# A hybrid decoder layer: state-space steps in another order, sample states from one product of 96 stacked rows

## The chip, the cores and the metric

The kernel runs on one core of a Trainium2 chip. A time is the device time of one execution in microseconds (us); a lower one is better. The engines are TensorE (PE; its weight loads are shown as PEld), VectorE (DVE), ScalarE (ACT), GpSimd (POOL) and SyncE (SP). Each takes its instructions in order, and they wait for one another by semaphores.

## What is computed

One layer of a decoder for a prompt of 512 tokens and 8 sequences of 8 new tokens each (64 sample tokens with a cache of 1024 positions and a state). Everything is fp32. Cut to what matters here:

```
h = rmsnorm(x);  q,k,v,z,xbc,dt,ga,gb = split(h @ w_in)
attn = stick_breaking_attention(q, k, v, cache)
xs,B,C = split(silu(causal_conv(xbc)))          # 32 heads of 64, 4 groups with 128 states each
per chunk of 128 tokens (samples: per sequence of 8):
    y_diag = (C B^T * L) (x dt)                 # L = exp of segment sums, lower triangle
    h      = h * decay + (x dt * decay_to_end)^T B
    y_off  = C h_before * exp(a_cum)
y = rmsnorm((y_diag + y_off + d_skip * xs) * silu(z), per group)
merged = sigmoid(ga) * (attn @ w_pa) + sigmoid(gb) * (y @ w_pb)
x = x + merged @ w_out;  x = x + (silu(h2 @ w_gate) * (h2 @ w_up)) @ w_down     # h2 = rmsnorm(x)
```

Among the outputs are the new states of the 8 sample sequences, `ssm_sample`: for each sequence, head and group, old state times decay plus the sum over its 8 tokens of `x dt decay` times `B`.

## The kernel before

The program is written as one stream of instructions for each engine, in the functions under `with` blocks for SP, POOL, PE, ACT and DVE; the order on each engine is the order of its Python code, and a table `keys`/`use` gives each product that is not a weight product one of four PSUM banks in turn (`spare`). All 576 tokens (512 + 64) go through each weight product at once.

A weight product keeps fp32 exactness by splitting: each operand is a hi part in fp32r and a lo part (the rest). `product` (L434 to L448) does three matmuls for each of two halves of 288 columns: w_hi x_hi (L443), w_hi x_lo (L444), w_lo x_hi (L447). One slice is 128 rows of the contraction, six matmuls; a tile is eight slices for 128 output columns, and a chunk of weights is one tile (two for w_pb). For each chunk ACT makes the hi part (L411) and DVE the lo part (L417).

The stages are: projections of q, k, v; attention, with the projections of the gates and some z tiles as filler (`Z_EARLY` lists the z tiles made there, kept in DRAM and brought back); w_pa; then the state-space part (from 483 us), w_out and the feed-forward part. The state-space part goes over four groups g of 8 heads. `by_token(g)` on PE transposes the convolved xs into five token blocks (`x_tok`, L1258; DVE makes `xdt` = x dt from each, L2291), B into `b_tok`, and forms C B^T (`cb`); slices of one weight tile (`key_after`, called `around` by the caller) stand between these. Then come the steps c = 0 to 3, one for each chunk of the prompt, and c = NC (4) for the samples. In a prompt step PE does:

- `segments` (L1292, L1293, L1300): segment sums by a product with picks; ACT takes exponentials (L1856) into `decay`;
- `old_and_state`: L1311 is the part of the output from the old state; L1318 the chunk's new state from `xend` (x dt decay_to_end, made by DVE at L2323);
- `new_outputs` (L1329): the output from the same chunk, from `decay` times C B^T (DVE, L2316) and `xdt`;
- `turn_old` (L1340) and twice `sequence(g, b)`: L1349 is the output of sample sequence b from its old state (8 columns), L1357 the addition to its state, which multiplies `xend_s` (64 sample tokens) by `b_seq[:, b]`, B with all tokens zero but those of b. `b_seq` is made by POOL (L882), `xend_s` by DVE (L2307). Before, this product is plain fp32.

Between these stand slices of filler tiles. `ssd_plan(g)` lists for each step two lists of tiles, and at its end those around the gate's sums of squares (`y_ss`, L1408): tiles of z (`z`), of the next group's inputs (`into`) or of w_pb for the group before (`pb`, two weight tiles in one). `step_tiles` makes `one` and `two` of them. With two tiles, four slices of `one` stand before `old_and_state` and four after it, and two of `two` at each of the four places behind. With one tile, three slices stand before, and one at each of the five places behind.

After a group, y is gated by z, squared (ACT), summed (PE, L1408) and scaled (DVE); ACT makes its hi part `y_hi` (L1937), DVE its lo part `y_lo` (L2426), from which the w_pb tiles of the next group's steps read. Behind the last group PE transposes the convolution's last rows (`conv_out`, L1422), which ACT copies out, and does the last w_pb tiles (`last_pb`); DVE then forms `merged` (L2439 to L2446).

On DVE, `prepare(g, c)` is what the change moves most. It waits until ACT has read both segment banks, multiplies `decay` by C B^T, then makes `xend`:

```
wait_after_read(eng, ("seg", g, c, q))          # q = 0, 1
eng.tensor_tensor(decay[...], decay[...], cb_m[...], ALU.mult)      # L2316
eng.tensor_tensor(xend[...], xdt[:, c], end_decay[...], ALU.mult)   # L2323
```

## Time and profile before

| | |
|---|---|
| median of 3 runs | 1569.98 us (1564.76, 1569.98, 1571.89) |
| profiled execution | 1569.13 us, its span 1567.6 us |
| PE busy | 1471.1 us, 94% of the span |
| DVE, ACT, POOL busy | 816.9, 635.5, 214.4 us |
| mean granted clock of TensorE | 0.971 |

The page says of which engine the busy time is; the views by stretch add the mean granted clock of the same stretch (1.00 is the full clock, 0.50 half of it). In the timelines, a row is an instruction or several alike in a row: its start, its time (start of the first to end of the last), engine, line, and in brackets how long the engine stood idle before it and for whom. Times of neighbouring matmuls overlap; the distance between starts is the time that each takes from PE.

### The profile page before, as it was taken

Reading aid. Unit: us, or ns where it says so; the run is one execution under the profiler, and the core shown is the slowest. Engines: PE = TensorE matmul, PEld = TensorE weight load, DVE = VectorE, ACT = ScalarE, POOL = GpSimd, SP = SyncE. Lnnn points to the kernel's source line nnn. Section 1 sums busy time; section 2 is a strip of 40 time slices with the busy share of each in tenths; the row PEclk is TensorE's granted clock in tenths of the full one; section 3 lists DMA queues with packets and bytes.
Section 4 is the critical chain, followed back from the end, with each engine's and each line's share of the span. In section 5 each row is a group of like instructions: output and inputs, shape, how many; then the busy total and the mean of one; then the engine's idle time right before and its main releaser. Section 6 shows DMA issues by size and latency. Waiting matters only on the chain. (4 is left out here: it accounts for less than half of the span.)

```text
span 1567.6 us, 27375 instructions
## 1 busy us (share of the span) xinstructions
PE 1471.1 (94%) x10773; PEld 1376.9 (88%) x10773; DVE 816.9 (52%) x1174; ACT 635.5 (41%) x1049; POOL 214.4 (14%) x391
## 2 busy tenths in 40 slices
PE   4998999999899998999999999979999999999997
PEld 4997778888799887979988988869999999999997
DVE  3454556878723655567666674546444444442221
ACT  4574446666513424534444353233433332322121
POOL 3011231000112122122112212111200000000001
PEclk9999999999999998899999999989999999999999
DMA  4235673222375232333333424354222322223331
GB/s 111 82 97 152 187 216 98 64 64 64 91 187 122 83 102 74 96 95 101 82 103 103 107 61 115 86 154 145 68 82 80 93 80 80 80 80 92 95 97 46
DMA packets 201110, 157.37 MB, mean 100 GB/s; under 512 B 13672, under 2 KB 187216, under 8 KB 200959
## 3 DMA queue, kind: packets, MB, share of 16 engines
q1 hardware_dynamic: 175394, 97.93, 22.1%
q0 software_dynamic: 25232, 57.70, 13.2%
q8 instruction: 67, 1.10, 0.3%
q10 hardware_dynamic: 384, 0.37, 0.1%
q14 instruction: 33, 0.27, 0.1%
HBM read 132.04 MB, written 23.91 MB: 99 GB/s over the span
## 5 line engine op out<-in xcount | busy, mean ns | idle before, releaser
L443 PE MATMUL tile_banks<-x_hi,w_hi 128*128 128x288 f32 (+1 forms) x1808 | 537.4, 311 | 20.1 <-ACT gate_out L1686 14.4
L444 PE MATMUL tile_banks<-x_lo,w_hi 128*128 128x288 f32 (+1 forms) x1808 | 512.1, 298 | 0.0
L447 PE MATMUL tile_banks<-x_hi,w_lo 128*128 128x288 f32 (+1 forms) x1808 | 391.2, 298 | 0.0
L443 PEld LDWEIGHTS tile_banks<-x_hi,w_hi 128*128 128x128 f32 (+1 forms) x1808 | 344.8, 191 | 36.9 <-issue 26.5
L444 PEld LDWEIGHTS tile_banks<-x_lo,w_hi 128*128 128x128 f32 (+1 forms) x1808 | 345.3, 191 | 4.8 <-issue 3.6
L417 DVE TENSOR_TENSOR w_lo<-w_raw,w_hi 128x1024 fp32r<-128x1024 f32 (+2 forms) x169 | 206.8, 1224 | 172.7 <-ACT w_hi L411 171.6
L447 PEld LDWEIGHTS tile_banks<-x_hi,w_lo 128*128 128x128 f32 (+1 forms) x1808 | 293.8, 190 | 0.4
L411 ACT ACTIVATE w_hi<-w_raw 128x1024 fp32r<-128x1024 f32 (+2 forms) x169 | 175.7, 1039 | 104.7 <-PE tile_banks L447 104.4
L443 PE MATMUL tile_banks<-f_hi,w_hi 128*128 128x288 f32 x352 | 99.4, 297 | 0.0
L444 PE MATMUL tile_banks<-f_lo,w_hi 128*128 128x288 f32 x352 | 98.5, 295 | 0.0
L443 PE MATMUL tile_banks<-y_hi,w_hi 128*128 128x288 f32 x256 | 79.8, 326 | 8.7 <-DVE merged L2439 8.7
L447 PE MATMUL tile_banks<-f_hi,w_lo 128*128 128x288 f32 x352 | 75.6, 296 | 0.0
L444 PE MATMUL tile_banks<-y_lo,w_hi 128*128 128x288 f32 x256 | 74.7, 306 | 0.0
L444 PEld LDWEIGHTS tile_banks<-f_lo,w_hi 128*128 128x128 f32 x352 | 66.3, 188 | 0.0
L443 PEld LDWEIGHTS tile_banks<-f_hi,w_hi 128*128 128x128 f32 x352 | 66.2, 188 | 0.0
L1800 ACT ACTIVATE conv_src<-tile_banks 128x288 f32<-128x288 f32 x24 | 9.9, 411 | 138.8 <-PE tile_banks L447 138.8
L1986 ACT ACTIVATE f_hi<-prod 128x576 f32 (+1 forms) x22 | 15.1, 686 | 119.9 <-DVE prod L2477 119.9
L443 PEld LDWEIGHTS tile_banks<-y_hi,w_hi 128*128 128x128 f32 x256 | 50.8, 198 | 14.3 <-DVE w_lo L417 9.1
L944 POOL DMA_DIRECT2D out_y_prompt<-y_tok x8 | 6.3, 785 | 416.4 <-ACT y_tok L1999 416.4
L2255 DVE SCALAR_TENSOR_TENSOR conv_acc<-conv_src,conv_par,conv_acc 128x600 f32<-128x600 f32 x72 | 60.8, 844 | 2.5
L447 PEld LDWEIGHTS tile_banks<-f_hi,w_lo 128*128 128x128 f32 x352 | 56.4, 188 | 0.0
L447 PE MATMUL tile_banks<-y_hi,w_lo 128*128 128x288 f32 x256 | 56.3, 302 | 0.0
(355 smaller groups left out, 2470.7 us busy)
## 6 DMA issues: line engine op xcount, KB each, us to landing
w_raw<-in_w_in SPq DMA_DIRECT2D x68, 512.0 KB, 4.0
w_raw<-in_w_gate SPq DMA_DIRECT2D x22, 512.0 KB, 3.8
w_raw<-in_w_up SPq DMA_DIRECT2D x22, 512.0 KB, 3.9
k_page<-in_cache_k SPq DMA_DIRECT2D x64, 128.0 KB, 2.6
v_page<-in_cache_v POOLq DMA_DIRECT2D x64, 128.0 KB, 2.9
old<-in_state_ssm POOLq DMA_DIRECT2D x32, 256.0 KB, 3.4
out_ssm_sample<-old POOLq DMA_DIRECT2D x32, 256.0 KB, 2.7
w_raw<-in_w_pb SPq DMA_DIRECT2D x16, 512.0 KB, 4.0
```

What stands on the lines that cost most here:

```text
L411: nc.scalar.activation(w_hi[:, c % 2, 0:tiles, 0:width], w_raw[:, c % 2, 0:tiles, 0:width], ACT.Copy).then_inc(hi_made, 1)
L417: nc.vector.tensor_tensor(w_lo[:, c % 2, 0:tiles, 0:width], w_raw[:, c % 2, 0:tiles, 0:width], f32(w_hi[:, c % 2, 0:tiles, 0:width]), ALU. ...
L443: nc.tensor.matmul(out, wh, xh[:, HALVES[h]], start=start and k == 0, stop=False, skip_group_check=onto)
L444: nc.tensor.matmul(out, wh, xl[:, HALVES[h]], start=False, stop=False, skip_group_check=onto)
L447: mm = nc.tensor.matmul(out, wl, xh[:, HALVES[h]], start=False, stop=stop and k == last, skip_group_check=onto)
L944: eng.dma_start(y_prompt[0].rearrange("(c p) n -> p c n", p=P)[:, :, bass.ds(P * i, P)], y_tok[:, 0:NC, :]).then_inc(sem("y_out"), 16)
L1800: eng.activation(dst[:, 3:3 + HALF], G[t % 2][:, 0, 0:HALF], ACT.Copy)
L1986: eng.activation(f_hi[:, bass.ds(2 * i + n, 1), :], prod2[:, n:n + 1, :], ACT.Copy).then_inc(sem("f_hi_made"), 1)
L2255: ins = eng.scalar_tensor_tensor(out=dst, in0=src[:, w:w + m], scalar=conv_par[:, w * CT + ct:w * CT + ct + 1], in1=dst, op0=ALU.mult, op1 ...
```

## The change

Two sets of edits go together.

1. **Sample states.** B of the samples and `xend_s` are split into hi and lo parts of fp32r and stacked on 96 partitions: 32 sample tokens (four sequences) three times, B as hi, hi and lo, `xend_s` as hi, lo and hi (lo, hi and hi for the second four), so one product of 96 rows gives the three partial products' sum. ACT makes the hi parts of B by six copies of 32 rows, DVE the lo parts by two subtractions; POOL's `spread_b` makes `b_seq` for four sequences at a time, so twice in a group (the second at c = 2, after the fourth sequence's product). `xend_f` is the fp32 product, ACT copies its hi parts (`xend_hi`, four copies of 32x512 behind the segments of c = 0), DVE subtracts (`xend_lo`, two of 32x512 behind the outputs of c = 0).
2. **Order.** `make_xend` is taken out of the end of `prepare`: for c = 0 it stands in `by_token` behind the second xdt, for the others at the start of `prepare`. Four slices of `around` stand before `by_token` instead of two, then 2, 1 and 1 between. `Z_EARLY` and `ssd_plan` share out z and w_pb tiles anew: in group 0, z(0,2) is made at c = 0 and c = 1 has two tiles; after groups 1 and 2 one z tile fewer is done; in the last group pb2 stands before the sums of squares and pb3 behind them. The last group's y_hi and y_lo have buffers of their own (over y_t and z_s). `a_seq` is made earlier on POOL, in the space of `conv_out`, and `picks` is narrower by one block.

```
-    Z_EARLY = [(0, 1), (0, 2), (1, 2), (1, 3), (2, 2), (2, 3)]
+    Z_EARLY = [(0, 1), (1, 2), (1, 3), (2, 1), (2, 2), (2, 3)]
...
 # ssd_plan: g == 0
-   [([z[3]], [into[0]]), ([into[1]], []), ([into[2]], []), ([into[3]], []), ([into[4]], [into[5]]), ([("z",1,0)], [("z",1,1)])]
+   [([z[2]], [into[0]]), ([z[3]], [into[1]]), ([into[2]], []), ([into[3]], []), ([into[4]], [into[5]]), ([("z",1,0)], [("z",1,1)])]
 # g = 1, 2: the last entry
-   ([pb[3]], [("z", g + 1, 0), ("z", g + 1, 1)])
+   ([pb[3]], [("z", g + 1, 0)])
 # g = 3
-   [([z[2]], []), ([z[3]], [pb[0]]), ([], [pb[1]]), ([], [pb[2]]), ([], []), ([pb[3]], [])]
+   [([z[1]], []), ([z[2]], [pb[0]]), ([z[3]], []), ([pb[1]], []), ([], []), ([pb[2]], [pb[3]])]
...
 # POOL, spread_b(g, n), called with n = 0 before the steps and n = 1 at c == 2
+   eng.tensor_tensor(b_seq[:, :, :], f32(b_hl[:, n, :]).unsqueeze(1).to_broadcast([3 * ROWS, SEQS, P]),
+                     in_seq_3[:, :].unsqueeze(2).to_broadcast([3 * ROWS, SEQS, P]), ALU.mult)
...
 # PE, by_token
-   gemm(key_after, {1: range(2, 4), 3: range(4, 6), 4: range(6, 8)}[c])
+   gemm(key_after, {1: range(4, 6), 3: range(6, 7), 4: range(7, 8)}[c])
 # PE, sequence
-   mm = pe.matmul(spare(key)[:, j * P:(j + 1) * P], xend_s[:, 2 * j:2 * j + 2, :]..., b_seq[:, b, :], ...)
+   mm = pe.matmul(spare(key)[:, j * P:(j + 1) * P], xend_s[:, b // SEQS, 2 * j:2 * j + 2, :]..., b_seq[:, b % SEQS, :], ...)
 # PE, end of a group
-   for key in later[:-1]:
+   for key in later if last else later[:-1]:
        gemm(key)
-   around = later[-1] if later else None
-   gemm(around, range(0, 2))
+   around = None if last else later[-1]
+   gemm(around, range(0, 4))
...
 # ACT, by_token and xend_hi
-   eng.activation(b_tok[0:TS, NC, :], spare(key)[0:TS, 0:P], ACT.Copy)
+   for n in range(2):
+       for k in (2, 1, 0):
+           ins = eng.activation(b_hl[k * ROWS:(k + 1) * ROWS, n, :], spare(key)[n * ROWS:(n + 1) * ROWS, 0:P], ACT.Copy)
...
+       for at in (n * ROWS, 2 * ROWS):
+           ins = eng.activation(xend_s[at:at + ROWS, n]..., rows, ACT.Copy)
 # ACT, sequence
+   if b == 1:
+       eng.wait_ge(sem("xend_s_made"), g + 1)
...
 # DVE, prepare
+   if 0 < c < NC:
+       make_xend(g, c)
    (waits for the segments, decay times C B^T)
-   if c < NC:
-       eng.tensor_tensor(xend[:, :, :], xdt[:, c], end_decay[...], ALU.mult)
```

The three places below show the order that the engines' streams have; the names are the tiles, as in `out<-in`.

DVE, `by_token` of group 1 and the decay product of its step c = 0, before:

```order
L2291 TENSOR_TENSOR xdt<-spare_bank,dt_tok 128x512 [waits bank_full0,y_split,bank_read0,conv_done]
L2291 TENSOR_TENSOR xdt<-spare_bank,dt_tok 128x512 [waits bank_full1]
L2291 TENSOR_TENSOR xdt<-spare_bank,dt_tok 128x512 [waits bank_full2]
L2291 TENSOR_TENSOR xdt<-spare_bank,dt_tok 128x512 [waits bank_full3]
L2291 TENSOR_TENSOR xdt<-spare_bank,dt_tok 64x512 [waits bank_full0]
L2295 TENSOR_SCALAR y_t<-xs_t,par 128x576 x4
L2299 TENSOR_TENSOR cb_m<-spare_bank,upto 128x512 [waits bank_full2]
L2303 TENSOR_TENSOR cb_m<-spare_bank,upto_b 64x64 [waits b_tok_made]
L2307 TENSOR_TENSOR xend_s<-xdt,end_decay 64x512 [waits bank_full0,bank_read0]
L2316 TENSOR_TENSOR decay<-decay,cb_m 128x1024 [waits bank_read2,bank_read1,bank_read0]
L2323 TENSOR_TENSOR xend<-xdt,end_decay 128x512 [waits bank_full1,bank_read0]
```

The same place in the changed kernel (`old_t` in its tenth row is the space that `xend_f` takes):

```order
L2336 TENSOR_TENSOR xdt<-spare_bank,dt_tok 128x512 [waits bank_full1]
L2324 TENSOR_TENSOR xend<-xdt,end_decay 128x512 [waits bank_full1,bank_read0]
L2336 TENSOR_TENSOR xdt<-spare_bank,dt_tok 128x512 [waits bank_full2]
L2336 TENSOR_TENSOR xdt<-spare_bank,dt_tok 128x512 [waits bank_full3]
L2336 TENSOR_TENSOR xdt<-spare_bank,dt_tok 64x512 [waits bank_full0]
L2342 TENSOR_SCALAR y_t<-xs_t,par 128x576 x4
L2346 TENSOR_TENSOR cb_m<-spare_bank,upto 128x512 [waits bank_full2]
L2352 TENSOR_TENSOR b_hl<-spare_bank,b_hl 32x128 [waits b_hi_made]
L2352 TENSOR_TENSOR b_hl<-spare_bank,b_hl 32x128
L2354 TENSOR_TENSOR cb_m<-spare_bank,upto_b 64x64
L2358 TENSOR_TENSOR old_t<-xdt,end_decay 64x512 [waits bank_full0,bank_read0]
L2379 TENSOR_TENSOR decay<-decay,cb_m 128x1024 [waits bank_read2,bank_read1,bank_read0]
```

xend moved from behind the decay product to behind the second xdt, and two subtractions stand ahead of the sample part.

PE, `by_token` of group 1, between the fourth and the fifth transposition of x_tok (L1258), before:

```order
L443 MATMUL tile_banks<-x_hi,w_hi 128x288
L444 MATMUL tile_banks<-x_lo,w_hi 128x288
L443 MATMUL tile_banks<-x_hi,w_hi 128x288
L444 MATMUL tile_banks<-x_lo,w_hi 128x288
L447 MATMUL tile_banks<-x_hi,w_lo 128x288 x2
L443 MATMUL tile_banks<-x_hi,w_hi 128x288
L444 MATMUL tile_banks<-x_lo,w_hi 128x288
L443 MATMUL tile_banks<-x_hi,w_hi 128x288
L444 MATMUL tile_banks<-x_lo,w_hi 128x288
L447 MATMUL tile_banks<-x_hi,w_lo 128x288 x2
L1258 MATMUL spare_bank<-ident,xs_t 64x128 [waits bank_read0]
L1258 MATMUL spare_bank<-ident,xs_t 64x128 x3
```

The same place in the changed kernel:

```order
L451 MATMUL tile_banks<-x_hi,w_hi 128x288
L452 MATMUL tile_banks<-x_lo,w_hi 128x288
L451 MATMUL tile_banks<-x_hi,w_hi 128x288
L452 MATMUL tile_banks<-x_lo,w_hi 128x288
L455 MATMUL tile_banks<-x_hi,w_lo 128x288 x2
L1279 MATMUL spare_bank<-ident,xs_t 64x128 [waits bank_read0]
L1279 MATMUL spare_bank<-ident,xs_t 64x128 x3
```

One slice instead of two stands ahead of the fifth transposition, which waits until DVE has read the first one's bank.

PE, the end of the last group, from the last sum of squares (L1408), before:

```order
L1408 MATMUL spare_bank<-conv_acc,ones 128x288 [waits y_squared]
L1408 MATMUL spare_bank<-conv_acc,ones 128x288
L1422 MATMUL spare_bank<-ident,conv_out 27x128 [waits bank_read3,conv_tails]
L1422 MATMUL spare_bank<-ident,conv_out 27x128 x3
L1422 MATMUL spare_bank<-ident,conv_out 27x128 [waits bank_read0]
L1422 MATMUL spare_bank<-ident,conv_out 27x128 x3
```

The same place in the changed kernel:

```order
L1429 MATMUL spare_bank<-conv_acc,ones 128x288 [waits y_squared]
L1429 MATMUL spare_bank<-conv_acc,ones 128x288
L451 MATMUL tile_banks<-y_hi,w_hi 128x288 [waits tile_free0,y_split,weights_split]
L452 MATMUL tile_banks<-y_lo,w_hi 128x288
L451 MATMUL tile_banks<-y_hi,w_hi 128x288
L452 MATMUL tile_banks<-y_lo,w_hi 128x288
```

The two tiles of pb3 now stand between the sums of squares and the transposes of the convolution's rows.

## Rows read from the trace of the kernel before

**Rows 1.** Stretches of groups 0, 1 and 3: busy time by engine, granted clock.

```profile
core 0: us, PE busy (x) PEld busy (x) DVE busy (x) ACT busy (x) POOL busy (x), PEclk, DMA share, GB/s
546.70:677.90 131.20, 122.74 (x789) 107.95 (x788) 76.03 (x127) 56.40 (x95) 25.90 (x43) 0.87 0.31 86
677.90:806.70 128.80, 125.07 (x933) 114.24 (x931) 85.06 (x138) 56.26 (x95) 25.38 (x43) 1.00 0.37 99
...
936.00:1073.00 137.00, 121.42 (x834) 108.66 (x834) 78.06 (x128) 45.67 (x67) 28.61 (x43) 0.91 0.43 128
```

**Rows 2.** PE's waits, 470 to 1075 us: total us, times, longest us.

```profile
PE spare_bank L1318 <- DVE xend L2323: 9.3, 9, 2.7
PE tile_banks L443 <- DVE merged L2439: 8.7, 2, 6.0
PE tile_banks L443 <- DVE w_lo L417: 4.5, 2, 2.3
PE spare_bank L1422 <- ACT xdt L1943: 4.2, 1, 4.2
PE spare_bank L1258 <- ACT xs_t L1773: 3.8, 1, 3.8
PE spare_bank L1216 <- POOL e_t L854: 2.6, 1, 2.6
PE spare_bank L1258 <- DVE xdt L2291: 2.5, 1, 2.5
```

**Rows 3.** Short stretches around falls of the clock; columns as in rows 1.

```profile
580.32:583.73 3.41, 3.41 (x28) 3.27 (x29) 2.26 (x6) 0.00 (x0) 0.00 (x0) 1.00 0.30 82
583.73:590.55 6.82, 6.82 (x24) 4.97 (x23) 2.90 (x8) 2.44 (x5) 2.77 (x5) 0.50 0.39 115
617.86:621.28 3.42, 3.13 (x8) 2.13 (x8) 0.74 (x2) 0.00 (x0) 0.00 (x0) 0.50 0.00 0
628.10:641.76 13.66, 13.66 (x55) 12.16 (x55) 7.02 (x14) 5.99 (x11) 2.93 (x6) 0.50 0.33 93
1030.88:1037.70 6.82, 5.79 (x26) 5.49 (x27) 3.68 (x5) 4.41 (x8) 2.09 (x4) 0.50 0.11 22
```

**Rows 4.** Timeline of PE, end of a slice and one sample sequence: start, us.

```profile
560.65 0.43 PE L447 MATMUL tile_banks<-x_hi,w_lo 128*128 128x288 f32 x2
560.92 0.95 PE L1349 MATMUL spare_bank<-bc_t,old_t 128*128 128x8 f32 x8
561.80 1.16 PE L1357 MATMUL spare_bank<-b_seq,xend_s 64*128 64x128 f32 x8
562.88 0.40 PE L443 MATMUL tile_banks<-x_hi,w_hi 128*128 128x288 f32 x1
```

**Rows 5.** Timeline of PE in attention, fp32r products of 128 columns.

```profile
278.12 0.22 PE L1164 MATMUL tile_banks<-wt_hi,v_hl 128*128 128x128 f32 x1
278.17 0.28 PE L1164 MATMUL tile_banks<-wt_lo,v_hl 128*128 128x128 f32 x1
278.29 0.44 PE L1164 MATMUL tile_banks<-wt_hi,v_hl 128*128 128x512 f32 x1
```

**Rows 6.** Timeline of all engines, group 0, step c = 3.

```profile
616.17 1.23 DVE L2316 TENSOR_TENSOR decay<-decay,cb_m 128x1024 f32<-128x1024 f32 x1 [2.46 <-ACT decay L1856]
...
617.32 0.68 DVE L2323 TENSOR_TENSOR xend<-xdt,end_decay 128x512 f32<-128x512 f32 x1
...
618.15 1.19 PE L1318 MATMUL spare_bank<-xend,b_tok 128*128 128x512 f32 x1 [2.74 <-DVE xend L2323]
```

**Rows 7.** Groups of instructions by form: count, busy us, mean ns, idle before.

```profile
L1824 ACT ACTIVATE b_tok<-spare_bank 64x128 f32<-64x128 f32 x4 | 1.1, 270 | 2.2 <-PE spare_bank L1277 2.2
...
L2307 DVE TENSOR_TENSOR xend_s<-xdt,end_decay 64x512 f32<-64x512 f32 x4 | 9.4, 2361 | 0.0
...
L882 POOL TENSOR_TENSOR b_seq<-b_tok,in_seq 64x1024 f32<-64x1024 f32 x4 | 7.6, 1888 | 77.7 <-ACT b_tok L1824 52.7 <-issue 25.0
```

**Rows 8.** Timeline of DVE, the last group's y_lo.

```profile
1030.58 2.76 DVE L2426 TENSOR_TENSOR y_lo<-y_t,y_hi 128x576 fp32r<-128x576 f32 x4
```

More of the change, by code:

```diff
@@ L503, in last_sums, with y_parts @@
             return ("e", g, c) if c else ("seg", g, c, 1)
+        def y_parts(g):
+            return (y_hi, y_lo) if g < NG - 1 else (y_last_hi, y_last_lo)
         def src_tile(key):
@@ L751, in _ @@
             rule(in_seq[:, :], 1.0, [(ge, 0, [[-TD, NB]], 1), (ge, TD - 1, [[TD, NB]], -1)], 0.0)
+            for k in range(3):
+                put(eng.tensor_copy, in_seq_3[k * ROWS:(k + 1) * ROWS, :], in_seq[0:ROWS, 0:SEQS])
             sem_const_all.append(n_made[0])
@@ L1241, in gemm @@
                         w = [a[:, c % 2].rearrange("p t n -> p (t n)")[:, cols] for a in (w_hi, w_lo)]
-                        x = (y_hi[:, k, :], y_lo[:, k, :])
+                        x = [y[:, k, :] for y in y_parts(key[1])]
                     else:
@@ L1832, in pick_group @@
                     eng.activation(sums[0:2 * NH, TP:T], one[:, 0:TS], ACT.Copy)
-                    for e in range(2):
-                        other = T + e * P + (1 - e) * HD
-                        eng.activation(picks[0:2 * NH, other:other + HD], one[:, 0:HD], ACT.Copy, scale=0.0).then_inc(sem("sums_filled"), 1)
-                    eng.wait_ge(sem("sums_filled"), 2)
+                    eng.activation(picks[0:2 * NH, T + HD:T + P], one[:, 0:HD], ACT.Copy, scale=0.0).then_inc(sem("sums_filled"), 1)
+                    eng.wait_ge(sem("sums_filled"), 1)
                     eng.wait_ge(sem("sums_split"), 4)
@@ L2280, in empty, with make_xend @@
                         ins.then_inc(tile_free[(t + n) % 2], 1)
+            def make_xend(g, c):
+                wait_after_read(eng, ("x_tok", g, c))
+                n = g * NC + c
+                if n:
+                    wait_full(eng, ("state", (n - 1) // NC, (n - 1) % NC))
+                eng.tensor_tensor(xend[:, :, :], xdt[:, c], end_decay[:, c, g * HG:(g + 1) * HG].unsqueeze(2).to_broadcast([P, HG, HD]), ALU.mult)\
+                   .then_inc(sem("xend_made"), 1)
             def by_token(g):
@@ L2301, in by_token @@
                 key = ("sample_bc", g)
-                eng.wait_ge(sem("b_tok_made"), g + 1)
+                eng.wait_ge(sem("b_hi_made"), g + 1)
+                low = slice(2 * ROWS, 3 * ROWS)
+                for n in range(2):
+                    ins = eng.tensor_tensor(b_hl[low, n, :], spare(key)[n * ROWS:(n + 1) * ROWS, 0:P], f32(b_hl[low, n, :]), ALU.subtract)
+                ins.then_inc(sem("b_split"), 1)
                 eng.tensor_tensor(cb_m[0:TS, NC, 0:TS], spare(key)[0:TS, P:P + TS], upto_b[:, :], ALU.mult).then_inc(bank_read[use[key][0]], 1)
@@ L2306, in by_token, with xend_lo @@
                     wait_full(eng, ("new_state", g - 1, NB - 1))
[L2307 to L2308 removed]
+                eng.tensor_tensor(xend_f.rearrange("p (h d) -> p h d", h=HG), xdt[0:TS, NC],
+                                  end_decay[0:TS, NC, g * HG:(g + 1) * HG].unsqueeze(2).to_broadcast([TS, HG, HD]),
+                                  ALU.mult).then_inc(sem("xend_f_made"), 1)
+            def xend_lo(g):
+                eng.wait_ge(sem("xend_hi_made"), g + 1)
+                for n in range(2):
+                    rows, other = slice(n * ROWS, (n + 1) * ROWS), slice((1 - n) * ROWS, (2 - n) * ROWS)
+                    flat = [x.rearrange("p h d -> p (h d)") for x in (xend_s[other, n], f32(xend_s[rows, n]))]
+                    ins = eng.tensor_tensor(flat[0], xend_f[rows, :], flat[1], ALU.subtract)
+                ins.then_inc(sem("xend_s_made"), 1)
             def prepare(g, c):
                 m = P if c < NC else TS
+                if 0 < c < NC:
+                    make_xend(g, c)
                 for q in range(2):
@@ L2317, in prepare @@
                    .then_inc(sem("decay_made"), 1)
-                if c < NC:
-                    wait_after_read(eng, ("x_tok", g, c))
-                    n = g * NC + c
-                    if n:
-                        wait_full(eng, ("state", (n - 1) // NC, (n - 1) % NC))
-                    eng.tensor_tensor(xend[:, :, :], xdt[:, c], end_decay[:, c, g * HG:(g + 1) * HG].unsqueeze(2).to_broadcast([P, HG, HD]), ALU.mult)\
-                       .then_inc(sem("xend_made"), 1)
             def outputs(g, c):
@@ L2425, in _ @@
                     eng.wait_ge(sem("y_hi_made"), PG * g + j + 1)
-                    ins = eng.tensor_tensor(y_lo[:, j, :], y_t[:, j, :], f32(y_hi[:, j, :]), ALU.subtract)
+                    high, low = y_parts(g)
+                    ins = eng.tensor_tensor(low[:, j, :], y_t[:, j, :], f32(high[:, j, :]), ALU.subtract)
                 ins.then_inc(sem("y_split"), 1)
```

83 lines of the change are left out of this document (53 added, 30 removed).

## The prediction, made before the changed kernel was run

> **What bounds the kernel now.** I read the stretches of the four state-space groups first, since all but one of the edits lie there. TensorE (PE) is the bound: in the stretch of group 0 it is busy 122.74 of 131.20 us, and in that of group 1 125.07 of 128.80 [rows 1]. So PE loses time in three ways: in waits, in the time its own instructions take, and in the granted clock. The clock column shows the last: 0.87 in group 0 and 0.91 in the last group, but 1.00 in group 1 [rows 1]. The levels are 2.4 and 1.2 GHz, so 0.87 over 131.20 us means 2 x 0.13 x 131.20 = 34 us at half speed, which costs 17 us; 0.91 over 137 us means 25 us, which costs 12. Second, PE's waits [rows 2]: the largest is 9.3 us in nine waits of L1318 (a chunk's new state) for xend, which VectorE (DVE) makes behind the decay product. Third, the low stretches [rows 3]. Some come behind a wait, as at 617.86. Others do not: from 580.32 to 583.73 PE is busy in all 3.41 us at 1.00, and the next 6.82 us run at 0.50 with PE busy throughout. That happens in steps with one filler tile, where the 8-column products of L1349 and the 64-row products of L1357 stand closest together. The stretch at 583.73 is one of three alike; the one at 628.10 is 13.66 us long.
>
> **The product of the sample states (L1357).** It is 4 fp32 matmuls for each of 8 sequences in 4 groups, and each matmul leaves two records. In the timeline the first of 8 records starts at 561.80 and the next tile's slice at 562.88 [rows 4]: 1.08 us for a sequence, 0.135 a record. The new form is 4 fp32r matmuls of 128 columns with 96 rows, one record each. No row shows 96 rows. The nearest are the fp32r products of the same 128 columns in attention: a 128-column one starts at 278.12, the next at 278.17, and a 512-column one at 278.29 [rows 5], so 0.05 and 0.12 us. I take 0.11, near the upper, because here the weights change with each matmul as at 278.17; it is also what an 8-column record at L1349 takes, (561.80 - 560.92)/8 = 0.11 [rows 4]. So 4 x 0.11 = 0.44 us, and the saving is (1.08 - 0.44) x 32 = **20.5 us**. The bounds: nothing faster per record than 0.135 gives 17.3 us; 0.05 gives 28. The work is on PE's path, so what it saves is seen unless a wait takes it. The Trainium skill's page "TensorE: Matmul & The Clock Gate" (section "Back-to-back issue gap") states about 81 ns a matmul for a stream of 128-column matmuls each with its weight load; by that figure an estimate is 0.32 us a sequence and 24 us in all. The two rows stand on both sides of it.
>
> **xend moved ahead of the decay product.** At 616.17 DVE starts the decay product (1.23 us), 2.46 us late because ScalarE (ACT) made the exponentials; xend follows at 617.32, and PE starts L1318 at 618.15 after a wait of 2.74 [rows 6]. xend needs neither. Moved ahead, it is ready long before, and L1318 would start at 615.41. PE then has one slice of six matmuls (0.135 each, 0.8 us [rows 4]) behind L1318's 0.55 and waits at L1329 for the decay product, which ends at 617.4 (by 616.17 + 1.23): 617.4 - 616.75 = 0.65 us. The other eight waits come to 6.6 us, 0.8 each; there the decay product, which now starts with the exponentials and no later than before, ends before PE has done L1318 and its slices. At c=0 of groups 1 to 3 I leave 0.9 in two of them, because there more work stands ahead of it (below). So of 9.3 us some 2.5 stay: **-6.8**.
>
> **What is added in a group.** ACT copies the hi parts of B in six instructions of 32x128 instead of one of 0.270 us [rows 7], so by that row some 1.35 us more stand ahead of the exponentials of c=0; its four copies for xend come after these and ahead of the next weight chunk. DVE has two small subtractions in by_token and two of 32x512 after the outputs of c=0; the step's xend of 0.685 us now lies between the second and third xdt. GpSimd (POOL) makes b_seq in two halves. Before, its one instruction of 1.888 us lies beside DVE's xend_s, which takes 2.361 although a full 128x512 product takes 0.68 (617.32 in [rows 6]); the two slow each other. POOL's first half is half as long; the second half comes at c=2, where I charge DVE up to 1 us, hidden by a step's slices. That half waits on POOL for the fourth sequence's product; queued behind it are the next sums and the old states of c=3, which are wanted a step later. ACT's copy for the second sequence waits for the split of xend, with c=0's slices between. DVE is busy 76 of 131 us and ACT 56 [rows 1], so I cost all this at nothing outside by_token and c=0. There the cover is the slices of `around` and of one or two tiles; if that cover is gone each group pays up to 2 us. The Trainium skill's page "SBUF — State Buffer" (section "Who interferes with whom") says that a DVE instruction with two SBUF inputs and a GpSimd instruction that reads SBUF exclude each other for a whole instruction. The trace agrees (2.361 beside 1.888 [rows 7]); by it the second half costs DVE about 1 us, and the sum would not change as long as DVE is not late there.
>
> **The start of a group.** Two more slices stand ahead of the first transposes of x_tok and one fewer between the fourth and the fifth. In group 0 the wait of 3.79 us for xs_t (L1258, [rows 2]) has 1.6 us more work ahead of it: -1.7 with rounding. In group 1 the wait of 2.45 for xdt shrinks by 1.6 - 0.8: -0.8. In groups 2 and 3 the end of the group before loses a whole tile of 6.4 us, and the fifth transposition will wait for DVE as long as the two waits for w_lo (4.5 in all [rows 2]) do now: zero. Sum **-2.5**. a_seq made early is worth little: the wait of 2.6 at L1216 is put down to it, but ACT's signed sums, on which the same product depends, come hardly earlier. **-0.5**, at most 2.6.
>
> **The end of the last group.** Before, the tile pb3 stands ahead of the sums of squares, and behind them PE has only the convolution rows' transposes, which wait 4.23 us at L1422 [rows 2]; around that the clock is at 0.50 for 6.82 us with 5.79 busy [rows 3], which costs 2.9. Now pb3's 6.4 us stand behind the sums, and the whole chain of the gate starts 6.4 us earlier. y_hi and y_lo get buffers of their own, so they need not wait for pb3. DVE's y_lo (2.76 us from 1030.58 [rows 8]) then would end at 1026.9, and the low part of the next weights, 1.2 us after it, sets the first tile of last_pb at about 1028.6, where it was 1033.5. **-5**; bounds 0 and 4.23 + 2.9 = 7.1. Next late there is the old wait for `merged` (8.7 us in two, [rows 2]), which the change leaves.
>
> **The clock.** The stretch at 617.86 goes with its wait: -1.7. That at 583.73 is in step c=1 of group 0, which has a second tile now: -3.4. The other one-tile stretches (6.8 for 628.10, 3.4 each for the other two) may stay or go: the steps are as they were, but the product that ran in them is shorter and the slices stand closer. I take half: -6.8. Sum **-12**; bounds: the whole 29 us of the two columns gone (17 + 12, of which the tail's 2.9 is counted above), and a clock that is worse than now.
>
> **The sum.** -20.5 - 6.8 - 2.5 - 0.5 - 5 - 12 = -47.3. The profiled execution took 1569.13 us (span 1567.6, the rest lies around it), the median of the runs is 1569.98. 1569.13 - 47.3 = 1521.8, and against the median 1522.7: **1523 us**.
>
> **Rivals.**
> (a) The clock is not regained: the one-tile steps keep what they have, or fall in all seven (there are two in group 0, one each in groups 1 and 2, three in group 3) for 6.82 us each. That is 7 x 3.4 = 24 us instead of the 17 of now: with the waits' own 1.7 regained, 1523 + 10 to 1523 + 17, so 1533 to 1540. For it: 583.73, where a wholly busy PE fell. Against it: the clock of 1.00 in group 1, whose step c=0 has one tile too. The Trainium skill, "TensorE: Matmul & The Clock Gate" (section "What's actually happening"), has the level follow how busy the array has been recently. By that rule removing waits raises the clock, and shorter products without more work behind them do not; the fall at 583.73 without a wait is not what its text alone leads one to expect.
> (b) ACT and DVE become the bound in by_token and at c=0. The six copies and the two subtractions delay the decay product by 2 us in each group: 1523 + 8 = 1531. For it: in before the exponentials already come 2.46 us late once [rows 6].
> (c) The product's price is the bound of either side: 0.135 a record gives 1526, 0.05 gives 1516.
> (d) The change does not do what it says with the waits: each simply moves from L1318 to L1329, and the by_token gain goes: 1523 + 9 = 1532.
> (e) The other side: with the fp32 product gone, every one of the 16 prompt steps runs low for 13.66 us as at 628.10. That costs 16 x 6.83 = 109 us against 17 in such steps now, +92, and leaves 1569 + 92 - 35 = 1626, slower. It decides from 17 + 35 = 52 us, that is, from eight of the 16 steps. Against it: nine steps have two tiles, and group 1 has a clock of 1.00 now.
>
> **How the numbers follow.** Forecast (1515 to 1530) 0.45; (a) 0.20; (b) 0.10; (c) 0.12, of which half below 1517; (d) 0.05; (e) 0.04; 0.04 for partial mixes that end within 0.5%, which is about what a measurement of this kernel can tell from no change. The low end takes in (c) at 0.05 with most of the clock back, 1505; the high end (a) with (b), 1546. Faster by over 0.5%: 0.92; within: 0.04; slower: 0.04.
>
> **What would show it.** L1357's successor has 128 records, about 0.11 us apart; if 0.135 or 0.05, (c). The waits of L1318 are gone, and L1329 waits under 1 us in a few places; if the waits are as large as before, (d); if L1329 waits about 2 us at c=0 of each group, (b). The 4.23 us at L1422 are gone, those for `merged` remain. The clock of group 0's stretch rises from 0.87 to about 0.93, with no low stretch in its step c=1; if it stays under 0.90, (a). The prediction is wrong in its core if PE's waits in the four groups do not fall by at least 10 us, or if the groups' clock falls.

## The result and the profile after

The changed kernel takes 1515.24 us (median of four runs, 1509.8 to 1519.96) where the kernel before takes 1570.93 in the same job: a ratio of 0.965 with a 95% interval of 0.9603 to 0.9697, 56 us less. A second set of runs of the same program gave 1512.63 us and 0.9653 (0.9612 to 0.9694). The prediction was 1523 us with a range of 1505 to 1546. The profiled execution took 1519.96 us, its span 1518.5, so 49 us less than the profiled one of before.

The changed kernel has other line numbers: L1318 (the new state from xend) is L1339, L1329 (the outputs that need the decay product) is L1350, L1258 is L1279, L1340 (the transposes of the samples' old states) is L1361, L1349 and L1357 are L1370 and L1378, L1422 is L1444.

The stretches of the four groups, each from its first segment sums to those of the next, the last one to the start of w_out (busy time by engine, granted clock; columns as in [rows 1]). The last row is the only stretch of over 7 us at half speed there:

```profile
541.04:652.02 110.98, 107.42 (x805) 97.05 (x803) 78.28 (x129) 61.45 (x105) 28.17 (x44) 1.00 0.38 106
652.02:768.74 116.72, 114.18 (x854) 104.21 (x852) 85.78 (x145) 58.86 (x102) 25.75 (x45) 0.99 0.38 108
768.74:885.08 116.34, 112.73 (x853) 102.97 (x852) 84.56 (x138) 59.22 (x103) 24.04 (x42) 1.00 0.36 100
885.08:1024.53 139.45, 125.80 (x842) 114.58 (x841) 80.75 (x135) 53.13 (x78) 28.81 (x44) 0.88 0.44 131
895.05:912.11 17.06, 16.91 (x67) 15.01 (x68) 6.49 (x14) 7.62 (x9) 3.63 (x5) 0.50 0.38 103
```

Group 0 took 131.20 us at a clock of 0.87 [rows 1] and takes 110.98 at 1.00, although it does a z tile more (z(0,2)). Groups 1 and 2 do one z tile less each (6.4 us of their 12 and 13). The last group gained nothing in this execution: its stretch went from 137.00 to 139.45, since a whole z tile moved into it and the clock fell to 0.50 for 17 us.

PE's waits from 470 us to the start of w_out (total us, times, longest us), to be read against [rows 2] and two smaller rows of the kernel before, which come first:

```profile
PE spare_bank L1349 <- DVE state L2361: 1.2, 5, 0.3
PE spare_bank L1329 <- DVE decay L2316: 1.0, 1, 1.0
```

```profile
PE tile_banks L451 <- DVE merged L2498: 9.4, 2, 6.4
PE spare_bank L1279 <- DVE xdt L2336: 5.4, 3, 1.9
PE spare_bank L1361 <- DMA old<-in_state_ssm: 3.4, 3, 1.9
PE spare_bank L1350 <- DVE decay L2379: 2.3, 4, 1.1
PE spare_bank L1244 <- ACT decay L1773: 2.2, 1, 2.2
PE spare_bank L1279 <- ACT xs_t L1795: 2.1, 1, 2.1
PE spare_bank L1370 <- DVE state L2417: 0.9, 4, 0.2
PE spare_bank L1339 <- DVE xend L2324: 0.9, 1, 0.9
PE tile_banks L451 <- DVE pb_sum L2315: 0.4, 1, 0.4
PE spare_bank L1339 <- ACT decay L1888: 0.4, 1, 0.4
PE spare_bank L1429 <- ACT conv_acc L1956: 0.2, 1, 0.2
```

The 9.3 us for xend are 0.9, the 4.2 us at the convolution rows are gone, the two waits for w_lo too. New is a wait of 3.4 us in three places for the old states of the samples (L1361). `merged` stays. All these waits together were 37.8 us and are 27.6.

The timeline of one sample sequence (start, us), as [rows 4] showed it before:

```profile
554.64 0.95 PE L1370 MATMUL spare_bank<-bc_t,old_t 128*128 128x8 f32 x8
555.45 0.64 PE L1378 MATMUL spare_bank<-b_seq,xend_s 96*128 96x128 f32 x4
555.92 0.35 PE L451 MATMUL tile_banks<-x_hi,w_hi 128*128 128x288 f32 x1
```

From the first record of the product to the next slice pass 0.47 us, where it was 1.08.

### The profile page after: what moved, and what is told of

Same layout as the page of the kernel before. It is cut to its first block and busy times, and to the rows that moved or that the text cites. A ratio compares the mean times of both kernels' runs of the same rounds, so it can differ in the third digit from the quotient of the medians.

```text
span 1518.5 us, 27179 instructions
## 1 busy us (share of the span) xinstructions
PE 1435.1 (95%) x10645; PEld 1348.8 (89%) x10645; DVE 823.0 (54%) x1190; ACT 654.2 (43%) x1086; POOL 217.2 (14%) x398
## 3 DMA queue, kind: packets, MB, share of 16 engines
q8 instruction: 66, 1.08, 0.3%
## 5 line engine op out<-in xcount | busy, mean ns | idle before, releaser
L451 PE MATMUL tile_banks<-y_hi,w_hi 128*128 128x288 f32 x192 | 57.6, 314 | 0.0
L777 POOL DMA_DIRECT2D v_page<-in_cache_v x64 | 34.5, 538 | 161.2 <-issue 161.2
L452 PE MATMUL tile_banks<-y_lo,w_hi 128*128 128x288 f32 x192 | 54.3, 298 | 0.0
L2162 DVE TENSOR_TENSOR_SCAN after_w<-rest,zero_col 128x128 f32<-128x128 f32 (+2 forms) x64 | 52.3, 818 | 0.3
```

What stands on the lines that cost most here:

```text
L451: nc.tensor.matmul(out, wh, xh[:, HALVES[h]], start=start and k == 0, stop=False, skip_group_check=onto)
L452: nc.tensor.matmul(out, wh, xl[:, HALVES[h]], start=False, stop=False, skip_group_check=onto)
L777: eng.dma_start(v_page[:, n % V_SLOTS, :], cache_v[0, bass.ds(page_of(eng, x, k), 1)].rearrange("o p h d -> p (o h d)")).then_inc(sem(f"v_ ...
L2162: link(eng.tensor_tensor_scan(out=after_w[:, slot, edge - width:edge][:, ::-1], data0=rest[:, slot, cols][:, ::-1], data1=zero_col[:, 0:1] ...
```

## Experiments

All times are medians; the kernels of one job share its runs of the kernel before (1567 to 1569 us). Each kernel has one profile, the changed kernel two. "Low" is the time at half clock between 500 and 1100 us of the profiled execution, the sum of its stretches; it was 65 us before and 38 after (24 in the second profile of the changed kernel).

### The two halves alone

The product alone: the kernel before with B and xend split, b_seq of 96 rows and

```
-   mm = pe.matmul(spare(key)..., xend_s[:, 2 * j:2 * j + 2, :]..., b_seq[:, b, :], ...)
+   mm = pe.matmul(spare(key)..., xend_s[:, b // SEQS, 2 * j:2 * j + 2, :]..., b_seq[:, b % SEQS, :], ...)
```

> The kernel before with the sample states by the fp32r product of 96 rows, and nothing else changed: xend behind the decay product, the old plans, the old end. Both theories: four records of 0.12 us for a sequence instead of eight of 0.135, so (1.08 - 0.47) x 32 = 19.5 us less on PE, and the old waits (L1318's 9.3 us in nine, 4.2 at the convolution's rows) as they were. Theory A (the fp32 products of 64 rows are what the clock falls behind in steps with one tile): the low stretches of group 0 that follow no wait (17 us at half speed there, 34 in all four groups, 17 us lost) go with them, in all 1571 - 19.5 - 15 = 1536 us, and the granted clock of group 0's stretch is 0.95 or more. Theory B (the steps with one tile themselves, or the waits in them): the stretches stay, 1571 - 19.5 = 1551 us, the clock of group 0 0.90 or less.

Measured: 1550.41 us against 1567.25, 0.9893 (0.9858 to 0.9927): 17 us less, as theory B had it, but not for its reason: the clock of group 0's stretch is 0.96, as theory A had it, and it is the waits that grew. The waits for xend (L1331 is L1318 here) and a few stretches:

```profile
PE spare_bank L1331 <- DVE xend L2364: 17.6, 8, 3.5
```

```profile
569.37:585.69 16.32, 15.17 (x115) 12.94 (x113) 11.42 (x21) 5.67 (x10) 5.09 (x8) 1.00 0.34 96
...
593.44:596.85 3.41, 2.79 (x6) 1.79 (x7) 1.07 (x2) 0.00 (x0) 0.85 (x2) 0.50 0.28 73
613.92:617.33 3.41, 3.04 (x7) 2.04 (x8) 0.82 (x2) 0.00 (x0) 0.00 (x0) 0.50 0.17 56
```

The waits for xend nearly doubled, from 9.3 to 17.6 us: PE comes to L1331 earlier, and xend still stands behind the exponentials and the decay product. At c = 0 it is also later, because six copies of B stand ahead of the exponentials on ACT:

```profile
548.05 1.66 ACT L1839 ACTIVATE b_hl<-spare_bank 32x128 fp32r<-32x128 f32 x6 [0.56 <-PE spare_bank L1290]
549.73 1.28 ACT L1879 ACT_TABLE_LOAD   x1
551.02 1.09 ACT L1879 ACTIVATE decay<-spare_bank 128x512 f32<-128x512 f32 x2
```

So 8 of the 19.5 us went straight into waits, and the clock fell at 593 and 614 around waits of 3.15 and 3.46 us, where before it had fallen in the steps. Group 0's stretches that follow no wait (583.73 in [rows 3]) are gone: step c = 1, the first row above, has the full clock. Low is 58 us in all.

The order alone: the changed kernel with the plain fp32 product.

```
-   eng.wait_ge(sem("b_split"), g + 1);  spread_b(g, 0)
+   eng.wait_ge(sem("b_tok_made"), g + 1);  (one b_seq of 64 rows x 8 sequences, as before)
```

> The changed kernel with the sample states as before (plain fp32 product of 64 rows, one b_seq for a group): order and plans alone. Both theories: L1318's waits fall from 9.3 us to under 3, those at the end of the last group and in by_token by 4 and 2.5, so 13 to 15 us less. Theory A: the stretches at half speed behind fp32 products in one-tile steps stay where a step still has one tile (group 0, c = 2 and 3: 20 us at half speed, so 10 lost), only that of c = 1 and the ones behind long waits go, 5 to 8 us: 1571 - 14 - 7 = 1550 us. Theory B: the waits were the cause, the clock comes back in all of them: 1571 - 14 - 17 = 1540 us, clock of group 0 0.95 or more. If the two edits add up, the two gains together are 56 us (1571 - 1515).

Measured: 1541.55 us, 0.9849 (0.9813 to 0.9886): 26 us less, between the theories (21 and 31 less). No wait for xend is left. But the clock of group 0's stretch is 0.90, and three long stretches at half speed begin in one-tile steps (c = 2 and 3 of group 0, c = 0 of group 1) with PE busy throughout and no wait over 0.26 us next to them; step c = 1 of group 0, which has two tiles here, keeps the full clock:

```profile
542.11:667.53 125.42, 123.15 (x838) 110.33 (x836) 75.54 (x125) 57.44 (x96) 24.97 (x43) 0.90 0.34 94
598.53:612.18 13.65, 13.65 (x51) 11.46 (x51) 7.08 (x15) 6.91 (x12) 4.54 (x8) 0.50 0.46 130
622.42:632.66 10.24, 10.24 (x40) 8.74 (x40) 5.12 (x10) 5.54 (x11) 2.92 (x6) 0.50 0.36 102
680.45:690.69 10.24, 10.24 (x36) 8.08 (x36) 6.79 (x12) 3.52 (x7) 4.50 (x8) 0.50 0.42 115
```

What follows from both: the halves give 17 and 26 us, together 43, and both at once 55 in the same job (1512.63). By the three intervals the 12 us on top can be about 2 to 22. The profiles show where each half alone hands something back: the product alone to waits for xend (8 us more of them, and low stretches around them), the order alone to low stretches in steps with fp32 products (48 us low, against 38 and 24).

### xend taken by itself, and put back

Alone, in the kernel before:

```
+   if 0 < c < NC:
+       make_xend(g, c)          # ahead of the decay product; c = 0 in by_token
    (waits, decay times C B^T)
-   eng.tensor_tensor(xend[:, :, :], xdt[:, c], ...)
```

> The kernel before with one edit: xend made ahead of the decay product (for c = 0 in by_token), all else as before, the sample product in plain fp32. Theory (the wait at L1318 was only for the place of xend on DVE): L1318's 9.3 us in nine waits fall under 1 us, L1329 waits up to 1 us in all, the low stretch behind the longest wait goes (1.7 us), those in one-tile steps stay, since the fp32 products of 64 rows are there: 9 + 2 = 11 us less, 1556 us from 1567. Rival: the wait moves to the decay product (L1329), and the time stays at 1567.

Measured: 1560.94 us, 0.994 (0.9917 to 0.9964): 8 us less. The wait at L1318 is gone in the trace and 0.6 us stand at L1329, so the rival falls: the wait does not move there (1.6 us for old states are new, at L1340 in group 2). The profiled execution, with 89 us low, was the slowest of its four (1571.16; the others 1558 to 1563). Group 0's one-tile steps ran low about as before (27 us of the 31 there), the first two rows; in the last group's steps 34 us were low where it had been 7, the third row for example:

```profile
603.63:613.87 10.24, 10.24 (x36) 8.08 (x36) 5.04 (x10) 6.44 (x12) 4.50 (x8) 0.50 0.45 126
624.11:634.35 10.24, 10.24 (x40) 8.74 (x40) 4.79 (x11) 5.07 (x11) 2.93 (x6) 0.50 0.38 108
982.51:996.16 13.65, 13.65 (x52) 11.47 (x52) 5.45 (x13) 2.73 (x4) 3.02 (x4) 0.50 0.38 112
```

In that execution all that the waits gave went back to the clock; the other three were 8 to 13 us faster than it. Why the last group ran low for longer is not shown. The same edit undone in the changed kernel:

> The changed kernel with xend made behind the decay product again, at the end of prepare. Theory (the two parts are worth more together: the shorter product and the added copies make PE wait longer for xend, as the product alone showed with 17.6 us of such waits): L1318's successor waits 15 to 18 us, five of the waits over 2.5 us, each with a low stretch of 3.4 us or more behind it (1.7 each, 8 in all): 1513 + 15 + 8 = 1536 us. Rival (the parts add up): it costs what xend's waits were before, 1513 + 7 = 1520 us.

Measured: 1531.61 us, 0.9759 (0.9723 to 0.9796): 16 to 19 us more than the changed kernel (1515.24 and 1512.63), with 15.4 us of waits for xend (eight, the longest 2.9), low 51 us. The theory of 1536 is nearer than the rival of 1520. By the medians the same move of one instruction on DVE is worth 8 us in the kernel before (6 to 13 by the interval) and 16 to 19 behind the shorter product (8 to 25); the waits that it removes, 9.3 and 15.4 us, say the same with less noise.

### What the clock falls behind

> The changed kernel with each fp32r product of the sample states done twice (the second overwrites the first with the same values), so that PE spends about as long at that place as with the plain fp32 product: 32 x 0.47 = 15 us more of work. Theory A (what the clock falls behind in one-tile steps is the fp32 product with its 64 rows, not the time that passes between slices): the clock of group 0's stretch stays at 0.97 or more, and the time is 1513 + 15 = 1528 us. Rival (the time between slices decides): stretches at half speed come back in the one-tile steps of groups 0 and 1, 20 to 34 us of them: 1513 + 15 + 10 to 17 = 1538 to 1545 us.

```
-   for j in range(PG):
+   for j in list(range(PG)) * 2:
```

Measured: 1524.06 us, 0.9738 (0.9708 to 0.9769), nearer theory A's 1528 than the rival's 1538 to 1545. Eight fp32r records take PE 0.92 us (556.18 to 557.10), close to the 1.08 of eight fp32 records, and group 0 keeps the full clock:

```profile
541.77:656.32 114.55, 111.01 (x837) 100.60 (x835) 78.28 (x129) 61.44 (x105) 28.18 (x44) 1.00 0.36 103
```

```profile
555.37 0.95 PE L1370 MATMUL spare_bank<-bc_t,old_t 128*128 128x8 f32 x8
556.18 1.09 PE L1378 MATMUL spare_bank<-b_seq,xend_s 96*128 96x128 f32 x8
557.10 0.35 PE L451 MATMUL tile_banks<-x_hi,w_hi 128*128 128x288 f32 x1
```

With the order the same, the fp32 product gave 0.90 and this one 1.00, so in group 0 it is not the time between slices. Over all kernels the clock of group 0's stretch sorts by the product: 0.87 before, 0.89 with xend alone, 0.90 with the order alone; with the fp32r product 0.96 where xend's waits are there (product alone, xend put back), and 0.98 to 1.00 in the others, but for 0.93 in the first of the two runs with the old end below, the one that leaves out slices. Its steps in group 0 are those of the changed kernel, and still its step c = 3 has a low stretch with no wait over 0.23 us in the step:

```profile
542.74:660.10 117.36, 112.60 (x794) 101.20 (x792) 80.00 (x133) 61.56 (x105) 26.75 (x44) 0.93 0.36 100
615.66:622.49 6.83, 6.83 (x27) 5.57 (x27) 4.59 (x9) 5.20 (x11) 2.59 (x6) 0.50 0.49 136
```

Whether it is the type or the 64 rows instead of 96 was not tried apart. Nor is the clock safe with the fp32r product in the last group, which has three one-tile steps. It ran low for 10 and 14 us in the run with the product twice, and for 10 us from 951 in the second profile of the changed one, with no wait over 0.43 us in the steps where that began; the order alone, with the fp32 product, has only 3.4 us low in that group's steps.

```profile
908.96:919.20 10.24, 10.24 (x38) 8.30 (x38) 4.30 (x8) 5.74 (x7) 3.36 (x5) 0.50 0.52 142
966.98:980.63 13.65, 13.04 (x66) 11.62 (x66) 8.51 (x17) 4.04 (x7) 2.27 (x3) 0.50 0.27 85
987.65:991.06 3.41, 3.41 (x15) 3.41 (x16) 3.26 (x6) 2.21 (x4) 0.75 (x1) 0.50 0.06 19
```

The first two rows are of the run with the product twice, the third of the order alone. So what sets the clock is shown for group 0 in part, and for the last group not at all. Over whole executions the mean granted clock was 0.970 to 0.982 with the order alone, 0.982 to 0.984 with the product twice and 0.975 to 0.986 in the changed kernel.

> The changed kernel with z(0,2) made as filler in attention again instead of z(2,1), so that step c = 1 of group 0 has one tile as before (and the end of group 1 has z(2,1)). Theory A (the fp32 products were what the clock fell behind): with the short product the one-tile step c = 1 keeps the full clock: 1513 us, within 3. Rival (the number of tiles decides): a low stretch of 6.8 us or more comes back in c = 1 of group 0, and waits of 1 to 2 us there: 1513 + 3.4 + 2 = 1518 us or more.

```
-   [([z[2]], [into[0]]), ([z[3]], [into[1]]), ...        # g == 0
+   [([z[3]], [into[0]]), ([into[1]], []), ...            # z(0,2) in Z_EARLY, z(2,1) at the end of group 1
```

Measured: 1510.62 us, 0.9645 (0.9608 to 0.9683), no difference from the changed kernel. With one tile again, step c = 1 keeps the clock:

```profile
544.24:649.00 104.76, 101.15 (x758) 90.66 (x756) 76.25 (x128) 60.40 (x104) 28.58 (x44) 1.00 0.38 107
```

So no worth of the sharing out of z tiles in group 0 shows once the product is short. Step c = 1 keeps the clock with either edit alone: with the second tile and the fp32 product in the order alone, with one tile and the fp32r product here and in the product alone.

### The end of the last group

> The changed kernel with the end of the last group as before: pb3 ahead of the sums of squares, y_hi and y_lo of the last group in the shared buffers (step c = 2 of that group takes z3 and pb1, c = 3 takes pb2). Theory: the 4.2 us wait at the convolution rows' transposes comes back with half speed around it: 4.5 to 7 us more, 1518 to 1520 us. Rival: pb3 only moved, and what waits behind it (the first w_pb tile of the last group, merged) takes the time: 1513 us, no change.

This kernel left out part of the work: two slices of one weight tile in each of three groups, 4.8 us. It took 1521.07 us (0.9675). The wait for DVE's xdt was 10.2 us in three, where the slices were missing, so its time doesn't answer the question. With them in place:

> As the run before with the end of the last group put back, but with every slice of the tile around by_token in place: that run left out two slices of one tile in three groups, 6 x 0.8 = 4.8 us of PE's work. Theory: the wait of 4.2 us at the convolution rows' transposes is there with half speed around it, and the changed kernel's waits are otherwise unchanged: 1513 + 4.5 to 7, so 1518 to 1520 us; with the clock as it was in the incomplete run up to 1526. Rival: nothing is gained by moving pb3: 1513 us.

```
-   ([z[3]], []), ([pb[1]], []), ([], []), ([pb[2]], [pb[3]])
+   ([z[3]], [pb[1]]), ([pb[2]], []), ([], []), ([pb[3]], [])
```

Measured: 1518.03 us, 0.9695 (0.9667 to 0.9724), 3 to 5 us more than the changed kernel; the intervals overlap (0.9612 to 0.9694 and 0.9603 to 0.9697), so the size is open, but the wait is back (L1435 is L1444 in the changed kernel):

```profile
977.40 1.91 PE L1435 MATMUL spare_bank<-ident,conv_out 128*27 128x128 f32 x16
983.53 1.91 PE L1435 MATMUL spare_bank<-ident,conv_out 128*27 128x128 f32 x8 [4.23 <-ACT xdt L1970]
```

### The new wait, and what is late next

> The changed kernel with the first two old states of a group loaded on POOL ahead of its wait for the split B, instead of behind the first half of b_seq. In the changed kernel PE waits 3.4 us in three places (0.2, 1.3, 1.86) at the transposes of the old states for these loads. Theory: they are late because they stand behind b_seq on POOL; then the waits go: 3.4 us less, and if the stretch at half speed that begins behind the longest of them (895.05 to 912.11) is its consequence, 8.5 us more: 1503 to 1512 us, clock of the last group's stretch from 0.88 to 0.94. Rival: the loads land no earlier since the states stored by the group before hold their buffers: no change, 1515 us, waits as they are.

```
+   for b in (0, 1):
+       old_states_in(g, b)
    eng.wait_ge(sem("b_split"), g + 1)
    ...
-       if c < NC:
+       if 0 < c < NC:
```

> The changed kernel once more, unchanged, as the ground for the others on the same chip: 1510 to 1520 us, ratio to before 0.960 to 0.970. If the stretch at half speed in step c = 0 of the last group comes by chance, it will be absent or shorter in this profile while the wait of 1.9 us ahead of it is there.

Measured in one job: 1505.45 us with the states first (0.9605, 0.9578 to 0.9631), 1512.63 unchanged (0.9653, 0.9612 to 0.9694). The wait at L1361 is gone from the trace. In the changed kernel PE stops there for what stands in POOL's queue: the first row is b_seq, which waits for the split of B, the second row the loads behind it.

```profile
887.83 1.03 POOL L873 TENSOR_TENSOR b_seq<-b_hl,in_seq 96x512 fp32r<-96x512 f32 x1 [19.03 <-issue]
889.15 1.54 POOL L869 DMA_DIRECT2D old<-in_state_ssm  x2 [0.29 <-POOL b_seq L873]
```

```profile
895.20 1.09 PE L1361 MATMUL spare_bank<-ident,old 128*128 128x128 f32 x4 [1.86 <-DMA old<-in_state_ssm]
```

In the kernel with the states first the loads stand at 869.46 and PE doesn't wait. The 7 us between the medians are more than the 3.4 us of waits; whether the stretch at half speed behind the 1.86 us is their consequence stays open: in the unchanged kernel's second profile the wait there was 0.2 us and the stretch was absent, which fits, but in the run with the product twice the wait there was 0.2 us as well, and 10 us of the same step ran low (908.96 above). The intervals of the two kernels overlap. With the states first the median is the lowest so far; the two below are no different from it.

> The changed kernel with the old states first, as above, and at the end of the last group the gates for the merge loaded on POOL ahead of the convolution rows' stores (whose last block goes to another buffer), so that DVE does not wait 4.0 us for gb_in. Theory: PE's wait for merged (8.2 us in two, 6.8 the longest) falls by 4 us, and the stretch at half speed of 10 us around it shrinks: 1505 - 4 - 2 = 1499 us. Rival: DVE's own chain of merged, hi and lo parts sets the pace, and the wait moves to the next tile: 1505 us.

> As the run before, with the gates of the second w_pb tile (n = 2 and 3) loaded on POOL ahead of x_again as well, since in that run DVE waited 5.2 us for gb_in of that tile, which stood behind x_again's 2.3 MB. Theory (the loads' place on POOL sets when the merge can go on): PE's waits for merged fall from 7.0 to about 2 us, the low stretch behind them (6.8 us) goes: 1505 - 5 - 3 = 1497 us. Rival: the time was set elsewhere, as the unchanged 1505 us of the run before says: 1505 us, the wait moves to the third tile or to x_again at the start of w_out.

Measured: 1505.21 us (0.9618, 0.9591 to 0.9645) and 1503.51 (0.9617, 0.9575 to 0.9658). In the first, the rival held: the first tile's wait for gb_in is gone on DVE, but the second tile's is 5.24 us, and PE's waits for merged are 7.0 us in two. In the second they fell to 4.7 us in three, less than hoped, and the third tile waits 2.84 us for its gb_in:

```profile
999.09 0.76 DVE L2507 TENSOR_TENSOR merged<-merged,gb_in 128x576 f32<-128x576 f32 x1 [2.84 <-DMA gb_in<-gates_dram]
```

The time did not move by more than its interval. The tile that waits is each time the one whose loads are the first behind those of x_again in POOL's queue: the second tile's at 984.99 us behind x_again at 983.71 in the first run, the third's at 990.83 behind 986.17 in the second. Whether x_again or the two buffers of gb_in hold them was not tried apart.

## Why the prediction held

**The sum.** Forecast -47.3, measured -49.1 between the profiled executions. PE was busy 1471.1 us and is 1435.1, 36.0 less, and idle (span less busy time) 96.5 and is 83.4, 13.1 less. Of the 36.0, the product is 19.5; the rest fits the clock, whose mean of 0.971 and 0.981 makes 91 and 58 us at half speed, so 16.5 given back. Against that stand the forecast's 20.5 for the product, 12 for the clock and 14.8 for the waits and the end. So in this execution each term is near, within 5 us. By the second profile of the same program (1507.18 us) the sum is -62, with more clock given back, so part of the nearness is the draw of the execution. The paragraphs below say where a term was near for another reason than the one given.

**The product.** Forecast 0.44 us a sequence, measured 0.47, so 0.61 x 32 = 19.5 us where 20.5 stood; the choice between the two rows was right, and both bounds (17.3 and 28) were further off. The 81 ns of the Trainium skill (page "TensorE: Matmul & The Clock Gate", "Back-to-back issue gap") would have been too short for this place: the records here stand 0.12 us apart.

**xend and what follows.** Forecast -6.8: L1318's and L1329's waits were 9.3 and 1.0 us and are 1.3 (0.9 for xend, 0.4 for the exponentials) and 2.3, together -6.7. That no wait would move to L1329 in full (rival d) is shown by the run with xend alone. What I did not see is that the value of this edit depends on the product: 8 us alone, 16 to 19 behind the shorter product. The sum came out right because both were done at once. My sign for the core, at least 10 us less of waits, was met by little: 37.8 us became 27.6 in this profile and 24.2 in the second, `merged` included.

**The start of a group.** Forecast -2.5: the waits for xs_t, xdt and w_lo were 10.8 us and are 7.5, -3.3. ACT's copies cost what was said (1.66 us for six), PE waits 0.36 to 0.43 us for the decay product at c = 0 of groups 1 to 3, not 0.9. a_seq: 2.6 us became 2.2, now for ACT's signed sums, -0.4, about as forecast.

**The end.** Forecast -5. From the start of the sums of squares to the first w_pb tile of the last group it was 11.7 us and is 13.5, of which 6.5 are pb3, so 4.7 less. With the end put back, the median is 3 to 5 us longer, within the intervals. The starts on PE, before (two rows) and after:

```profile
1021.76 4.18 PE L1408 MATMUL spare_bank<-conv_acc,ones 128*128 128x288 f32 x16
...
1033.47 0.59 PE L443 MATMUL tile_banks<-y_hi,w_hi 128*128 128x288 f32 x1
```

```profile
971.49 4.18 PE L1429 MATMUL spare_bank<-conv_acc,ones 128*128 128x288 f32 x16
975.29 0.51 PE L451 MATMUL tile_banks<-y_hi,w_hi 128*128 128x288 f32 x1
...
981.83 2.78 PE L1444 MATMUL spare_bank<-ident,conv_out 128*27 128x128 f32 x24
985.01 0.37 PE L451 MATMUL tile_banks<-y_last_hi,w_hi 128*128 128x288 f32 x1 [0.41 <-DVE pb_sum L2315]
```

**A step that was missing.** POOL's b_seq now waits for the split of B, and the old states of the group's first two sequences stand behind it in POOL's queue. I named what stands behind the second half and not what stands behind the first. It cost PE 3.4 us in this profile and 2.2 in the other. That PE comes earlier is part of it: with xend alone, where b_seq waits for no split, there are 1.6 us of it once, with the order alone 0.2.

**The clock.** This is the term that was mis-sized and whose cause was only half seen. Forecast -12 in all, with half of the one-tile stretches gone and group 0 at about 0.93; group 0 got back its whole 17 us (0.87 to 1.00), and the whole kernel 16.5 us in this profile and some 21 in the second (mean clock 0.984). In this profile 8.5 were lost again in the last group, in the stretch at 895.05; in the second profile of the same program that stretch is absent and one of 10 us at 951 stands instead, and such differences are part of the spread of the runs (1502 to 1523). So the 12 were too few by 4.5 and 9 us, and half of the one-tile stretches gone is not what happened: nearly all went in group 0, and others came in the last group. I gave the 3.4 us of step c = 1 to its second tile; the tile does keep the clock there with the old product, but so does the new product without the tile, so the tile was not needed. The halves show the rest: with the fp32 product the one-tile steps of group 0 ran low in all three profiles although PE was busy all the time (13.65 of 13.65 us), 24 to 27 us of them with no long wait next to them; with the fp32r product group 0 holds 0.93 or more. Rival (a) is refuted for group 0; in the last group it is not. The rule of the Trainium skill's page "TensorE: Matmul & The Clock Gate" ("What's actually happening"), by which the level follows how busy the array has been, does not tell the two products apart by PE's busy time in the profile; the traces of group 0 do, by which product fills it.

**The rivals.** (b) and (c) did not come about: L1350 waits 2.3 us in all, and the product lies between its bounds. (e), slower, did not come about either, though one-tile steps with PE wholly busy do run low: with xend alone 89 us were low instead of 65 in one execution, and the last group's steps with the fp32r product fell for 10 us and more.

## What to carry to other kernels

A move that takes a wait off the bounding engine and an edit that shortens that engine's work can be worth more together than apart, as here: shorten the work, and what stood a little behind it becomes late (9.3 us of waits for xend became 17.6), so ask of each such thing what it waits for. Where an instruction is given a new wait, list what stands behind it in its queue, the loads on a DMA queue's engine above all. And read the granted clock by stretch before costing small waits, since what the clock gives or takes (17 us in one group here) can be larger than the wait that is removed.

## What the runs showed of the hardware

- In group 0, steps with one filler tile and the fp32 product of 64 rows and 128 columns ran at half clock for 7 to 14 us at a time though PE was busy throughout (583.73 and 628.10 in [rows 3]; 598.53 and 622.42 with the order alone); with twice as many fp32r products of 96 rows, in about the same time (0.92 and 1.08 us), the clock of that group stayed at 1.00. In the last group of that run it fell all the same, for 10 and 14 us.
- The same program's runs spread over 1502 to 1523 us, and its two profiles, 12.8 us apart, differ in where and how long the clock was low (38 and 24 us, so 7 of the 12.8) and in waits.
- DVE's product of 64x512 with two inputs beside POOL's b_seq took 1.50 us (1.49 to 1.55) in the changed kernel beside POOL's 1.03, and 2.361 beside 1.888 before [rows 7]: against the 0.68 of a 128x512 product [rows 6] that is 0.8 and 1.7 us longer, most of POOL's time. That agrees with the lock that the Trainium skill describes in "SBUF — State Buffer", section "Who interferes with whom".
